# Hybrid decoder trunk on one core: gate groups and branch projections token by channel, both layers written out, the merge transposed onto its old layout

## The chip, the cores and the metric

The kernel runs on one core of a Trainium2 chip. The metric is device time in microseconds (us) of one execution, the median of several runs. The engines are named as in the profile: PE (TensorE; PEld is its weight load), DVE (VectorE), ACT (ScalarE), POOL (GpSimd), SP (SyncE, which here issues nearly all DMAs).

## What is computed

256 tokens of width 1024 go through two layers and a last RMSNorm. Cut to what matters here:

```
for l in range(2):
    h = rms_norm(x, norm_mix_g[l])
    proj = h @ w_in[l]                      # 1024 x 7492: u, va, q, k, v, index, cb, cc, cx, six gate groups of 512
    ya = gmlp_spatial(u, va, ws, bs)        # 512 wide
    yb = dsa_attention(q, k, v, ...)        # top 64 keys of each query, 4 heads
    yc = cb * conv3(cc * cx)                # 512 wide
    g  = sigmoid(gates)                     # 3 x 1024
    merged = g[0] * (ya @ w_proj_a) + g[1] * (yb @ w_proj_b) + g[2] * (yc @ w_proj_c)
    x = x + merged @ w_out
    h = rms_norm(x, norm_ffn_g[l])
    x = x + hier_moe(h, ...)                # 32 experts, 1024 x 512 x 1024, two for each token
return rms_norm(x, norm_final_g)
```

All is float32. The products of the mixing part are made of three products of rounded parts (high times high, high times low, low times high).

## The kernel before

**One layer** has a mixing part, a router and an expert part, and each engine runs its own program for it, in a hardware loop over the layer (`Fori(0, DEPTH) as l`: L434 on SP, L562 on POOL, L582 on ACT, L797 on DVE, L1201 on PE). Since `l` is in a register, each wait on a semaphore counts up from a value that a register instruction works out.

**Weights.** `ring` has 12 slots of 1 MB. In mixing SP loads weights into seven of them (`MIX_RING`); a load waits until the product that read the slot seven loads before is done. ACT rounds each slot to its high part (`high`, L636, into four more slots), DVE subtracts that for the low part (`low`, L813). A high part waits until the product that read the one four before is done.

**Mixing on PE.** `group(g)` (L1247) makes one group of 512 columns of `w_in`, from two slots, over 8 chunks of the 1024 input channels. Groups go by turns to psA and psB. Two orientations are in use, told apart by `token_major` (L1248): the first five groups (index, q, k, v, va) hold a 128-token piece of `hT` in the array and stream 512 weight columns; u, cx, cc, cb and the six gate groups hold 128 weight columns and stream 256 tokens, so their result has channels on the partitions. In both a `product` (L1218) is three matmuls:

```
def product(o, xs, ws, weights_stationary, start, stop):
    for i, (a, b) in enumerate(TERMS):
        first, second = (ws[b], xs[a]) if weights_stationary else (xs[a], ws[b])
        ins = te.matmul(o, first, second, start=start and i == 0, stop=stop and i == len(TERMS) - 1)
    return ins
```

Between the groups stand the small products of attention and of the spatial gate. After the gate groups come six branch projections (`for k in range(N_PROJ)`, ya, yb, yc for the first 512 channels, then for the other 512), with the weights in the array and 256 tokens streamed. DVE multiplies each by its gate (L1013) and adds (L1016) into `merged`, 8 chunks of channels by 256 tokens. ACT rounds each half of it to `merged_high` (L645), DVE makes `merged_low` (L1002), and PE multiplies both with `w_out` (two parts of the sum times two halves of the columns), which DVE adds to `x` (L1031).

**Router and experts.** DVE works out the top groups and experts, PE makes ranks, and a table tells for each pair of experts which tokens it takes. An inner hardware loop (L1508 on PE, L1167 on DVE, L726 on ACT, L500 on SP) runs over the pairs of experts, 16 in each layer with these inputs. A pair reads 12 slots (12 MB): PE gathers tokens (L1427), multiplies with gate and up (L1439) and down (L1451), and scatters by a 0/1 matrix (L1465, L1466); DVE adds to `x` (L1117). SP loads the next pair's slot when PE has freed it (`pair_freed`), six stages of two slots to a pair.

**The end of a layer** on DVE: the last two additions to `x`, then the layer loop's register instruction and branch, then at the loop's head the sum of squares of the next layer's norm (L828).

Of the kernel before, what the change touches and what calls it, by code (L numbers as in the profile page):

```python
# [29 lines left out]
P = 128  # L30
# [20 lines left out]
def build_trunk(nc, x_in, positions, norm_mix_g, norm_ffn_g, norm_final_g, w_in, gmlp_ws, gmlp_b, conv_w,  # L51
                w_proj_a, w_proj_b, w_proj_c, w_out, router_group_w, router_group_b,
                router_expert_w, router_expert_b, expert_w_gate, expert_w_up, expert_w_down, out):
    _, S, D = x_in.shape
# [87 lines left out]
    with ExitStack() as ctx:  # L142
# [6 lines left out]
        def rounded(name):  # L149


            offset, shape = place[name]
            return nc.alloc_sbuf_tensor_at(name + "_parts", shape, F32R, offset=offset)
# [34 lines left out]
        k_tok = share1[:, 1024:2048].rearrange("p (t n) -> p t n", t=NT)  # L188
        merged = share1[:, :].rearrange("p (c s) -> p c s", c=KC)
        qT = xn[:, 0:1024].rearrange("p (h s) -> p h s", h=HEADS)  # L190
# [8 lines left out]
        hT_high = rounded("hT")  # L199
        merged_high, merged_low = hT_high, rounded("share1")[:, :].rearrange("p (c s) -> p c s", c=KC)  # L200
        xn_parts = rounded("xn")
# [6 lines left out]
        hid = share1[:, 1536:2048]  # L208
        gate_parts = rounded("gates")
        y_high, y_low = [gate_parts[:, i].rearrange("p m s -> p (m s)").rearrange("p (n w) -> p n w", n=2) for i in (0, 3)]  # L210
# [135 lines left out]
        branch_act = sem("branch_act")  # L346
        merged_act = sem("merged_act")
        act_out = sem("act_out")
        idxT_act = sem("idxT_act")
# [77 lines left out]
        def sync_program(sp):  # L427
# [5 lines left out]
            sp.dma_start(rows[DEPTH * KC:, :], conv_w.rearrange("l k (c p) -> (l k c) p", p=P)).then_inc(rows_landed, 16)  # L433
            with sp.Fori(0, DEPTH) as l:  # L434

# [98 lines left out]
        def pool_program(pool):  # L534
# [25 lines left out]
            for k in range(STAGES):  # L560
                gp.memset(credit[:, k:k + 1], 0.0).then_inc(pair_freed, 1)
            with pool.Fori(0, DEPTH) as l:  # L562

                pool.wait_ge(wsT_act, l + 1)
                alone(pool)
                gp.affine_select(out=wsT[:, :, :], in_=wsT[:, :, :], compare_op=ALU.is_ge, fill=0.0, base=0,
                                 pattern=[[0, HEADS], [1, P]], channel_multiplier=-1).then_inc(tri_done, 1)


        def scalar_program(act):  # L570
# [10 lines left out]

            with act.Fori(0, DEPTH) as l:  # L582
                act.wait_ge(pairs_known, l + 1)
# [59 lines left out]
                def merged_part(half):  # L643
                    act.wait_ge(merged_done, l * 2 + half + 1)
                    sc.activation(merged_high[:, 4 * half:4 * half + 4, :], merged[:, 4 * half:4 * half + 4, :],  # L645
                                  ACT.Copy).then_inc(merged_act, 1)

# [100 lines left out]
        def vector_program(dve):  # L748
# [47 lines left out]

            with dve.Fori(0, DEPTH) as l:  # L797
                linked = [0]
# [200 lines left out]
                def merged_part(half):  # L999
                    dve.wait_ge(merged_act, l * 2 + half + 1)  # L1000
                    part = slice(4 * half, 4 * half + 4)
                    v.tensor_tensor(merged_low[:, part, :], merged[:, part, :], merged_high[:, part, :],  # L1002
                                    ALU.subtract).then_inc(merged_low_dve, 1)
# [3 lines left out]
                for half in range(2):  # L1007
                    dst = merged[:, 4 * half:4 * half + 4, :].rearrange("p (b h) s -> p b (h s)", b=2)
                    t2 = tmp[:, :].rearrange("p (b n) -> p b n", b=2)
# [184 lines left out]
        def tensor_program(pe):  # L1194
# [5 lines left out]
            pe.wait_ge(setup_done, 1)  # L1200
            with pe.Fori(0, DEPTH) as l:  # L1201
                pe.wait_ge(pairs_known, l + 1)
# [43 lines left out]
                def group(g):  # L1246

                    token_major = g in (G_QI, G_Q, G_K, G_V, G_VA)  # L1248
                    n = N_IDX if g == G_QI else WB
# [116 lines left out]


                for k in range(N_PROJ):
                    n = N_IN + k
                    p = PAD + 2 * N_IN + k  # L1370
                    branch = k % 3
                    if k == 0:
                        pe.wait_ge(branch_low_dve, l * 3 + 3)
                    w = split(p)
                    free_result(n)
                    for m in range(4):
                        for c in range(4):
                            ins = product((psA, psB)[n % 2][:, m // 2, (m % 2) * S:(m % 2 + 1) * S],
                                          [part[:, c, :] for part in (branch_high[branch], branch_low[branch])],
                                          [wp[:, c, m * P:(m + 1) * P] for wp in w], True, c == 0, c == 3)  # L1380
                    ins.then_inc(mixed, 1)

                for part in range(2):
                    for half in range(2):
# [6 lines left out]
                        for t in range(NT):  # L1391
                            for c in range(4):
                                m = 4 * part + c
                                ins = product((psA, psB)[n % 2][:, t, :], [h[:, m, t * P:(t + 1) * P] for h in (merged_high, merged_low)],
                                              [wp[:, c, :] for wp in w], False, m == 0, m == KC - 1)
                        if part == 1:
                            ins.then_inc(mixed, 1)
# [158 lines left out]
```

## Time and profile before

| | us |
|---|---|
| median of 3 runs | 1511.23 (1511.0 to 1513.61) |
| the profiled execution, its device time | 1510.52 |
| its span, first to last instruction | 1508.4 |
| TensorE's mean granted clock in it | 0.981 |
| PE, DVE, ACT busy | 1428.3, 557.2, 423.8 |

The device time lies 2.1 us above the span of the same execution, and the median 0.7 us above that execution. In the chain of waits a row is: start in us, length in us, engine, what it writes and its line; "issue" is time in which the engine waited for nothing that the profile shows. In the timeline a row is: start, length, engine, line, operation, output, inputs, shapes, count, and in brackets idle time before it and who ended it.

### The profile page before, as it was taken

The page shows a single profiled execution, that of the slowest core. Times are in us where ns is not written, and L with a number is a line of the kernel's source. Part 1 is how long each engine was busy: PE and PEld are TensorE (multiplying, and loading weights), DVE is VectorE, ACT ScalarE, POOL GpSimd, SP SyncE. Part 2 cuts the span into 40 slices and gives each one's busy share as a digit, 9 for nine tenths or more (in the row PEclk, how much of TensorE's full clock was granted, in tenths as well). Part 3 has the DMA queues.
Part 4 walks back from the last instruction along what each step waited for, and adds up shares of the span by engine and source line. Part 5 has one row for each costly group of instructions (what it writes and reads, how often), then busy time and mean ns, then how long its engine had stood idle before and what let it go on. Part 6 is the DMA issues. An engine that isn't in the chain of part 4 may idle for free.

```text
span 1508.4 us, 22388 instructions
## 1 busy us (share of the span) xinstructions
PE 1428.3 (95%) x8295; PEld 902.0 (60%) x8296; DVE 557.2 (37%) x872; ACT 423.8 (28%) x531; POOL 7.4 (0%) x43
## 2 busy tenths in 40 slices
PE   6999999899999999999879999998999999999996
PEld 5899998544444444444368999985444444444443
DVE  6785355522212212221267754564222222221223
ACT  5544332312212212211254543332221221221121
POOL 1000000000000000000000000000000000000000
PEclk9999999899999999999989999998999999999999
DMA  7544354899999999999935344548999999999995
GB/s 268 186 157 168 129 207 168 326 420 422 421 423 421 421 423 421 421 422 422 403 122 177 135 154 159 203 162 359 419 422 422 422 422 422 421 422 422 421 422 219
DMA packets 100818, 489.31 MB, mean 324 GB/s; under 512 B 8686, under 2 KB 12054, under 8 KB 51608
## 3 DMA queue, kind: packets, MB, share of 16 engines
q1 hardware_dynamic: 99656, 488.20, 80.8%
q8 instruction: 36, 0.59, 0.2%
q10 hardware_dynamic: 1104, 0.34, 0.1%
q14 instruction: 22, 0.18, 0.0%
HBM read 487.46 MB, written 1.05 MB: 324 GB/s over the span
## 4 chain that ended last, share of the span: by engine, by line
PE 63%; DMA 25%; DVE 6%; issue 4%; ACT 1%; SPq 0%; DVEq 0%; POOL 0%; ACTq 0%; POOLq 0%
DMA ring<-in_expert_w_up_dram 25%; PE psB L1439 19%; PE psA L1218 14%; PE psB L1218 12%; PE psC L1451 8%; PE psA L1427 5%; PE psA L1465 1%; PE psA L1466 1%; DVE work L908 1%; DVE top L907 1%; DVE ring_parts L813 1%; PE psD L1493 1%; PE psC L1340 1%; PE psC L1408 0%; PE psC L1339 0%
## 5 line engine op out<-in xcount | busy, mean ns | idle before, releaser
L1439 PE MATMUL psB<-ring,share 128*64 128x512 f32 x2048 | 462.8, 597 | 18.4 <-DMA ring<-in_expert_w_up_dram 18.4
L1439 PEld LDWEIGHTS psB<-ring,share 128*64 128x64 f32 x2048 | 141.9, 137 | 291.6 <-issue 271.0
L1451 PE MATMUL psC<-ring,share 128*64 128x512 f32 x1024 | 226.8, 595 | 0.0
L813 DVE TENSOR_TENSOR ring_parts<-ring,ring_parts 128x2048 fp32r<-128x2048 f32 (+1 forms) x80 | 176.8, 2249 | 69.1 <-ACT ring_parts L636 68.1
L636 ACT ACTIVATE ring_parts<-ring 128x2048 fp32r<-128x2048 f32 (+1 forms) x80 | 146.9, 1878 | 63.3 <-PE psA L1218 40.1
L1451 PEld LDWEIGHTS psC<-ring,share 128*64 128x64 f32 x1024 | 70.7, 137 | 131.7 <-issue 127.9
L1427 PEld LDWEIGHTS psA<-gates,xn 128*128 128x128 f32 x1088 | 131.4, 198 | 27.7 <-issue 26.0
L1117 DVE TENSOR_TENSOR x<-x,psA 128x1024 f32<-128x1024 f32 x62 | 75.7, 1221 | 192.0 <-PE psA L1466 192.0
L1427 PE MATMUL psA<-gates,xn 128*128 128x128 f32 x1088 | 140.3, 284 | 1.6 <-DVE gates L1086 1.6
L1218 PE MATMUL psA<-ring_parts 128*128 128x256 f32 (+2 forms) x416 | 126.2, 303 | 0.0
L1131 DVE TENSOR_TENSOR gates_parts<-psC,gates_parts 128x512 fp32r<-128x512 f32 x64 | 41.2, 686 | 222.8 <-ACT gates_parts L737 222.8
L1218 PE MATMUL psA<-hT_parts,ring_parts 128*128 128x256 f32 x640 | 117.4, 286 | 5.3 <-DVE ring_parts L813 5.3
L1218 PE MATMUL psB<-hT_parts,ring_parts 128*128 128x256 f32 x640 | 120.5, 291 | 0.0
L1218 PE MATMUL psB<-ring_parts 128*128 128x256 f32 (+1 forms) x384 | 117.5, 306 | 0.0
L737 ACT ACTIVATE gates_parts<-psC 128x512 fp32r<-128x512 f32 x64 | 34.7, 595 | 262.9 <-PE psC L1451 262.9
L1218 PEld LDWEIGHTS psA<-hT_parts,ring_parts 128*128 128x128 f32 x640 | 100.8, 194 | 6.1 <-issue 6.1
L1218 PEld LDWEIGHTS psB<-hT_parts,ring_parts 128*128 128x128 f32 x640 | 103.4, 199 | 0.4 <-issue 0.4
L1127 DVE SCALAR_TENSOR_TENSOR share<-gates,psB 128x512 f32<-128x512 f32 x32 | 23.9, 747 | 198.0 <-PE psB L1439 197.6
L1110 DVE TENSOR_TENSOR share<-psA,g_ffn 128x512 f32<-128x512 f32 x68 | 47.0, 691 | 95.8 <-PE psA L1427 95.8
L1218 PEld LDWEIGHTS psA<-ring_parts 128*128 128x128 f32 x416 | 79.9, 192 | 2.5
L729 ACT ACTIVATE gates<-psD 64x1 f32<-64x1 f32 x64 | 10.6, 165 | 249.0 <-PE psD L1482 248.6
L1218 PEld LDWEIGHTS psB<-ring_parts 128*128 128x128 f32 x384 | 75.3, 196 | 2.5
(310 smaller groups left out, 1300.3 us busy)
## 6 DMA issues: line engine op xcount, KB each, us to landing
ring<-in_expert_w_gate_dram SPq DMA_DIRECT2D x128, 1024.0 KB, 20.3
ring<-in_expert_w_up_dram SPq DMA_DIRECT2D x128, 1024.0 KB, 21.4
ring<-in_expert_w_down_dram SPq DMA_DIRECT2D x128, 1024.0 KB, 20.0
ring<-in_w_in_dram SPq DMA_DIRECT2D x56, 1024.0 KB, 7.0
ring<-in_w_out_dram SPq DMA_DIRECT2D x8, 1024.0 KB, 5.6
ring<-in_w_proj_a_dram SPq DMA_DIRECT2D x4, 1024.0 KB, 6.6
ring<-in_w_proj_b_dram SPq DMA_DIRECT2D x4, 1024.0 KB, 6.1
ring<-in_w_proj_c_dram SPq DMA_DIRECT2D x4, 1024.0 KB, 6.2
```

The costliest lines, as they stand in the source:

```text
L636: sc.activation(high_and_low(p)[0], mix_slot(p), ACT.Copy).then_inc(high_act, 1)
L737: sc.activation(y_high[:, n, :], psC[:, n, :], ACT.Copy).then_inc(y_act, 1)
L813: v.tensor_tensor(low_part, mix_slot(p), high_part, ALU.subtract).then_inc(low_dve, 1)
L907: link(v.max(top8[:, :], left[:, 0:nk]), True)
L1110: v.tensor_tensor(xT[:, 4 * b:4 * b + 4, :], psA[:, b, :].rearrange("p (c n) -> p c n", c=4), g_ffn[:, 4 * b:4 * b + 4].unsqueeze(2).to_br ...
L1117: v.tensor_tensor(x[:, t, :].rearrange("p (b n) -> p b n", b=2), x[:, t, :].rearrange("p (b n) -> p b n", b=2), (psB if last and t else ps ...
L1127: v.scalar_tensor_tensor(hid, silu, slot_w, psB[:, 1, :], ALU.mult, ALU.mult).then_inc(hid_done, 1)
L1131: v.tensor_tensor(y_low[:, n, :], psC[:, n, :], y_high[:, n, :], ALU.subtract).then_inc(y_dve, 1)
L1218: ins = te.matmul(o, first, second, start=start and i == 0, stop=stop and i == len(TERMS) - 1)
L1427: ins = te.matmul(psA[:, b, (c % 4) * P:(c % 4 + 1) * P], xn[:, o:o + P], sel[:, t].rearrange("p j n -> p (j n)"), start=t == 0, stop=t == ...
L1439: ins = te.matmul(psB[j * BLK:(j + 1) * BLK, o, :], xT[:, 4 * half + c, j * BLK:(j + 1) * BLK], w[:, c, :], start=half == 0 and c == 0, st ...
L1451: ins = te.matmul(psC[j * BLK:(j + 1) * BLK, n, :], hidT[:, 2 * k + c, j * BLK:(j + 1) * BLK], w[:, c, n * 512:(n + 1) * 512], start=k == ...
```

## The change

The gate groups are made token by channel like the first five groups (a 128-token piece in the array, 512 weight columns streamed), and so are the six branch projections. `merged` then has tokens on its partitions. Since the products with `w_out` need channels there, PE transposes each half of `merged` with the identity matrix into psC and psD, eight transposes of 128x128 to a half: the first half behind the fourth projection, the second behind the first quarter of the `w_out` product. ACT and DVE take `merged_high` and `merged_low` from psC and psD, where they took them from `merged` in SBUF, and `merged_low` moves from the place of `merged` to that of two gates that are used up. On every engine the hardware loop over the layer is a loop of the program's text, so that both layers are written out and `l` is a constant; the loops over the pairs stay.

```
-            with sp.Fori(0, DEPTH) as l:
+            for l in range(DEPTH):
...
-            with pool.Fori(0, DEPTH) as l:
+            for l in range(DEPTH):
...
-            with act.Fori(0, DEPTH) as l:
+            for l in range(DEPTH):
...
                 def merged_part(half):
-                    act.wait_ge(merged_done, l * 2 + half + 1)
-                    sc.activation(merged_high[:, 4 * half:4 * half + 4, :], merged[:, 4 * half:4 * half + 4, :],
-                                  ACT.Copy).then_inc(merged_act, 1)
+                    act.wait_ge(merged_ps, l * 2 + half + 1)
+                    sc.activation(merged_high[:, 4 * half:4 * half + 4, :].rearrange("p (b c) s -> p b (c s)", b=2),
+                                  (psC, psD)[half][:, :, :], ACT.Copy).then_inc(merged_act, 1)
...
-            with dve.Fori(0, DEPTH) as l:
+            for l in range(DEPTH):
...
                 def merged_part(half):
                     dve.wait_ge(merged_act, l * 2 + half + 1)
-                    part = slice(4 * half, 4 * half + 4)
-                    v.tensor_tensor(merged_low[:, part, :], merged[:, part, :], merged_high[:, part, :],
+                    v.tensor_tensor(merged_low[half].rearrange("p (b c) s -> p b (c s)", b=2), (psC, psD)[half][:, :, :],
+                                    merged_high[:, 4 * half:4 * half + 4, :].rearrange("p (b c) s -> p b (c s)", b=2),
                                     ALU.subtract).then_inc(merged_low_dve, 1)
...
-                    dst = merged[:, 4 * half:4 * half + 4, :].rearrange("p (b h) s -> p b (h s)", b=2)
+                    dst = merged[:, :, 512 * half:512 * half + 512]
...
-            with pe.Fori(0, DEPTH) as l:
+            for l in range(DEPTH):
...
-                    token_major = g in (G_QI, G_Q, G_K, G_V, G_VA)
+                    token_major = g in (G_QI, G_Q, G_K, G_V, G_VA) or g >= G_GATE0
...
+                def merged_transposes(half):
+
+                    pe.wait_ge(merged_done, l * 2 + half + 1)
+                    for c in range(4):
+                        for t in range(NT):
+                            o = (c % 2) * S + t * P
+                            ins = te.transpose((psC, psD)[half][:, c // 2, o:o + P],
+                                               merged[:, t, (4 * half + c) * P:(4 * half + c + 1) * P], ident[:, :])
+                    ins.then_inc(merged_ps, 1)
+
                 for k in range(N_PROJ):
...
-                    for m in range(4):
+                    for t in range(NT):
                         for c in range(4):
-                            ins = product((psA, psB)[n % 2][:, m // 2, (m % 2) * S:(m % 2 + 1) * S],
-                                          [part[:, c, :] for part in (branch_high[branch], branch_low[branch])],
-                                          [wp[:, c, m * P:(m + 1) * P] for wp in w], True, c == 0, c == 3)
+                            ins = product((psA, psB)[n % 2][:, t, :],
+                                          [part[:, c, t * P:(t + 1) * P] for part in (branch_high[branch], branch_low[branch])],
+                                          [wp[:, c, :] for wp in w], False, c == 0, c == 3)
                     ins.then_inc(mixed, 1)
+                    if k == 3:
+                        merged_transposes(0)
...
-                                ins = product((psA, psB)[n % 2][:, t, :], [h[:, m, t * P:(t + 1) * P] for h in (merged_high, merged_low)],
+                                o = slice(t * P, (t + 1) * P)
+                                ins = product((psA, psB)[n % 2][:, t, :], [merged_high[:, m, o], merged_low[part][:, c, o]],
                                               [wp[:, c, :] for wp in w], False, m == 0, m == KC - 1)
+                        if part == 0 and half == 0:
+                            merged_transposes(1)
```

How the instructions stand, at two places. First PE at the end of the fourth branch projection (the first of the second half of the channels; `ring_parts` are the rounded weights, `xn_parts` and `uT_parts` the parts of ya, `share` is `merged`). Before, its last matmuls and the first of the fifth projection:

```order
L1218 MATMUL psA<-uT_parts,ring_parts 128x256
L1218 MATMUL psA<-xn_parts,ring_parts 128x256 x2
L1218 MATMUL psA<-uT_parts,ring_parts 128x256
L1208 REGISTER_ALU
L1228 REGISTER_ALU
L1218 MATMUL psB<-ybT,ring_parts 128x256 x2
```

and of the change:

```order
L1219 MATMUL psA<-ring_parts,uT_parts 128x512
L1219 MATMUL psA<-ring_parts,xn_parts 128x512 x2
L1219 MATMUL psA<-ring_parts,uT_parts 128x512
L1375 MATMUL psC<-ident,share 128x128 x8
L1219 MATMUL psB<-ring_parts,ybT 128x512 x2
L1219 MATMUL psB<-ring_parts,xn_parts 128x512
```

The matmuls are 512 wide and half as many, and the eight transposes stand between the two projections; the register instructions ahead of the waits are gone.

Second DVE from the last row of its pair loop to the norm that follows. Before (L797 is the layer loop's branch, and what follows it in the text is the norm after the last layer; the next layer's is at the loop's head):

```order
L1167 COMPARE_AND_BRANCH
L1117 TENSOR_TENSOR x<-x,psA 128x1024
L1117 TENSOR_TENSOR x<-x,psB 128x1024
L1173 ISA
L797 REGISTER_ALU
L797 COMPARE_AND_BRANCH
L1184 ISA xn,ss<-x 128x1024
```

and of the change, behind the first layer:

```order
L1168 COMPARE_AND_BRANCH
L1118 TENSOR_TENSOR x<-x,psA 128x1024
L1118 TENSOR_TENSOR x<-x,psB 128x1024
L1174 ISA
L829 ISA xn,ss<-x 128x1024
L829 ISA ss 128x1
L787 TENSOR_SCALAR var<-ss 128x2
```

The second layer's norm now stands directly behind the first layer's last addition, with no branch between them.

## Rows read from the trace of the kernel before

**Rows 1.** The page: span, and the chain that ended last by engine.

```profile
span 1508.4 us, 22388 instructions
...
PE 63%; DMA 25%; DVE 6%; issue 4%; ACT 1%; SPq 0%; DVEq 0%; POOL 0%; ACTq 0%; POOLq 0%
```

**Rows 2.** Chain of waits in the expert parts: start us, us, what.

```profile
349.26 7.02 PE psB L1439 x32
...
377.37 7.02 PE psB L1439 x32
...
1304.52 25.40 DMA ring<-in_expert_w_up_dram
...
1334.37 25.41 DMA ring<-in_expert_w_up_dram
```

**Rows 3.** Busy time of 284 to 288 us; columns PE, PEld, DVE, ACT, POOL, PEclk, DMA share, GB/s.

```profile
284.00:288.00 4.00, 4.00 (x21) 1.46 (x21) 0.69 (x1) 0.00 (x0) 0.00 (x0) 1.00 0.02 6
```

**Rows 4.** Timeline of SP's DMA issues: the second pair's first load.

```profile
288.36 1.03 SPq L445 DMA_DIRECT2D ring<-in_expert_w_gate_dram  x2
```

**Rows 5.** Chain of waits in the first mixing part: group q, two gate groups, a projection, a w_out quarter.

```profile
25.59 10.89 PE psB L1218 x48
...
159.89 13.59 PE psB L1218 x96
...
185.00 11.52 PE psB L1218 x96
...
219.45 5.65 PE psB L1218 x48
...
247.50 5.44 PE psA L1218 x24
```

**Rows 6.** Timeline of PE: group cx starts after idle time.

```profile
90.08 0.50 PE L1218 MATMUL psA<-hT_parts,ring_parts 128*128 128x256 f32 x2 [2.63 <-DVE ring_parts L813]
```

**Rows 7.** Timeline of ACT and DVE during the fourth gate group: high and low parts of two slots.

```profile
175.38 3.71 ACT L636 ACTIVATE ring_parts<-ring 128x2048 fp32r<-128x2048 f32 x2
...
177.32 4.50 DVE L813 TENSOR_TENSOR ring_parts<-ring,ring_parts 128x2048 fp32r<-128x2048 f32 x2 [0.58 <-ACT ring_parts L636]
```

**Rows 8.** Timeline of PE: eight transposes of q and the next group.

```profile
60.49 1.03 PE L1292 MATMUL psD<-ident,share 128*128 128x128 f32 x8
61.28 0.71 PE L1218 MATMUL psA<-ring_parts,hT_parts 128*128 128x512 f32 x2
```

**Rows 9.** Timeline of ACT and DVE at the merge: merged_high, last addition of the second half, merged_low.

```profile
229.02 1.06 ACT L645 ACTIVATE hT_parts<-share 128x1024 fp32r<-128x1024 f32 x1 [7.61 <-DVE share L1016]
...
243.33 1.23 DVE L1016 TENSOR_TENSOR share<-share,tmp 128x1024 f32<-128x1024 f32 x1
...
249.09 1.22 DVE L1002 TENSOR_TENSOR share_parts<-share,hT_parts 128x1024 fp32r<-128x1024 f32 x1
```

**Rows 10.** Chain of waits from the first layer into the second, on DVE.

```profile
750.48 1.23 DVE x L1117
...
751.89 5.59 issue
...
757.61 0.13 DVE xn L828
```

**Rows 11.** Chain of waits from the second layer into the last norm, on DVE.

```profile
1498.58 1.22 DVE x L1117
...
1500.04 0.11 DVE xn L1184
```

**Rows 12.** Timeline of ACT from the first layer into the second.

```profile
746.43 1.28 ACT L580 ACT_TABLE_LOAD   x1 [0.17 <-issue]
```

**Rows 13.** Chain of waits between two linked DVE instructions of the top-k scores.

```profile
57.20 0.03 issue
```

**Rows 14.** Busy time around the transposes of q and behind the spatial gate; columns as in rows 3.

```profile
60.00:64.00 4.00, 4.00 (x23) 3.38 (x22) 2.83 (x13) 3.31 (x3) 0.00 (x0) 1.00 0.50 135
160.00:164.00 4.00, 4.00 (x19) 4.00 (x20) 3.98 (x3) 0.00 (x0) 0.00 (x0) 0.50 0.02 4
```

More of the change, by code:

```diff
@@ L188, in build_trunk @@
         k_tok = share1[:, 1024:2048].rearrange("p (t n) -> p t n", t=NT)
-        merged = share1[:, :].rearrange("p (c s) -> p c s", c=KC)
+        merged = share1[:, :].rearrange("p (t n) -> p t n", t=NT)
         qT = xn[:, 0:1024].rearrange("p (h s) -> p h s", h=HEADS)
@@ L199, in build_trunk @@
         hT_high = rounded("hT")
-        merged_high, merged_low = hT_high, rounded("share1")[:, :].rearrange("p (c s) -> p c s", c=KC)
+        gate_parts = rounded("gates")
+        merged_high, merged_low = hT_high, (gate_parts[:, 0], gate_parts[:, 2])
         xn_parts = rounded("xn")
@@ L208, in build_trunk @@
         hid = share1[:, 1536:2048]
-        gate_parts = rounded("gates")
         y_high, y_low = [gate_parts[:, i].rearrange("p m s -> p (m s)").rearrange("p (n w) -> p n w", n=2) for i in (0, 3)]
@@ L347, in build_trunk @@
         merged_act = sem("merged_act")
+        merged_ps = sem("merged_ps")
         act_out = sem("act_out")
```

## The prediction

> **What bounds the kernel now.** I read the span and the chain by engine first [rows 1]: 1508.4 us, of which 63% is PE, 25% DMA, 6% DVE. The device time of this execution is 1510.52 us, the median 1511.23; all sums below are differences, so they apply to either.
>
> In the expert parts two paces show [rows 2]. While the ring still holds a reserve, a pair takes 377.37 - 349.26 = 28.11 us, set by PE. Later it takes 1334.37 - 1304.52 = 29.85 us, and the chain lies in the DMA of the twelve slots. The slower of the two, the DMA, decides the end. When does that stream start? The ring is full before the experts begin: from 284 to 288 us the DMAs move 6 GB/s [rows 3], and the next load is issued only at 288.36 us, when PE has freed the first stage of the first pair [rows 4]. So the end of a layer is PE's first expert product plus about 15 x 29.85 us and a tail. Whatever is gained before the experts moves the end by the same amount, and nothing that this change does inside the pair loops matters unless a pair grows past 29.85 us.
>
> In the mixing parts the chain runs on PE from group to group [rows 5]. A group of 48 matmuls, 512 wide, takes 10.89 us (0.227 us each); a gate group of 96, 256 wide, takes 11.52 us (0.120 us each). The columns are the same 24,576, so the difference of 0.63 us is what each matmul costs beside its columns. The one place where PE waits for another engine among the groups is before group cx, 2.63 us for DVE's low part, behind the top-k work [rows 6]; the change does not touch this chain of work.
>
> **The change, part by part.**
>
> *Gate groups.* Six in each layer go from 11.52 to 10.89 us [rows 5]: 12 x 0.63 = 7.6 us gained. ACT and DVE must keep up. The tightest place is the fourth gate group: the low parts for the fifth are ready at 177.32 + 4.50 = 181.8 us [rows 7], and the fifth starts at 185.00 [rows 5], 3.2 us later; with shorter groups 2.6 us are left. Sigmoid, gates and multiplications keep their sizes.
>
> *Branch projections.* 48 matmuls in 5.65 us become 24 as wide as those of a `w_out` quarter, 5.44 us [rows 5]: 12 x 0.21 = 2.5 us gained.
>
> *Transposes.* Eight between two groups cost 61.28 - 60.49 = 0.79 us from start to start [rows 8]. Four times eight are added, all on PE's path: 3.2 us lost. They bring two handovers. Take T as the end of the fourth projection. Before, the first half of `merged` is complete at 228.99 us (rounding starts at 229.02 [rows 9]), 1.7 us before the fourth projection ends (219.45 + 2 x 5.65 = 230.75, the second having ended at 219.45 [rows 5]); with projections 0.2 us shorter it stays 1.3 us early, so PE does not wait at T. Transposes end at T + 0.8, ACT's rounding (1.06) at T + 1.9, DVE's low part (1.22) at T + 3.1 [rows 9]. Queued behind them: ACT's high parts of two `w_out` slots (1.85 each [rows 7]) end at T + 5.6, DVE's low parts (2.25 each [rows 7]) at T + 8.3, then the products of the fifth projection, which has been ready since T + 6.2. Its multiplication and addition (1.23 each [rows 9]) end at T + 10.7, those of the sixth (ready at T + 11.7) at T + 14.2. PE reaches the second transposes after two projections and a quarter of `w_out`, at T + 0.8 + 3 x 5.44 = T + 17.1: 2.9 us of room. It needs the second low part at T + 23.4; DVE has two low parts of weights until T + 18.7, ACT's rounding ends at T + 19.0, the low part at T + 20.2: 3.2 us of room. If the cover were gone, a handover would cost 0.8 + 1.06 + 1.22 = 3.1 us each. I take 0.
>
> *The layer loop.* Once in the run, DVE goes back to the loop's head. Its last addition ends at 751.71 us; then come 5.59 us in which it waits for nothing, and the norm starts at 757.61 [rows 10]: 5.90 us. At the end of the second layer the same kind of norm stands straight behind the addition and starts at 1500.04, 0.24 us after 1499.80 [rows 11]. The difference, 5.7 us, is on the path, since everything of the second layer hangs on this norm. ACT goes round the same loop and loses 0.17 us [rows 12], so the loss depends on how much program an engine must go back over. In the change there is no way back: I take the 5.7 us as gained whole. The ends are 0 (the code of the second layer must be fetched anyway and might be late) and 5.7.
>
> *Register instructions.* On DVE 200 of them stand in the old text and 14 in the new. Between two linked instructions of the top-k work 0.03 us pass, with a register instruction between them [rows 13]; they run while the engine works. I take 0; the gain is at most the 0.03, times some 70 links on the path, 2 us.
>
> Sum: -7.6 - 2.5 + 3.2 - 5.7 = -12.6 us. The profiled execution would take 1497.9, the median 1498.6 us.
>
> **What the Trainium skill says, beside the rows.** The rows show 0.120 and 0.227 us from matmul to matmul [rows 5]. The Trainium skill, page "TensorE: Matmul & The Clock Gate", section "Back-to-back issue gap", gives columns over 2.4 GHz plus 2.5 ns, so about 0.109 and 0.216 us. By that a gate group would gain only 0.1 us; it is the third rival. The trace does not agree with it in size, and the trace has both forms in this very code, so I go by the trace.
>
> **The rivals.**
>
> 1. *The stall on DVE stays in another place.* The second layer's code is new text, and its first instructions might arrive late behind the pair loop. For it: nothing but the stall's own size. Against it: the last norm, also behind a pair loop, came in 0.24 us [rows 11]. Then -6.9 us: 1504.3 us.
>
> 2. *The transposes cost PE its clock.* Behind the spatial gate, with its many small matmuls, the granted clock is 0.50 (1.2 GHz) at 160 to 164 us [rows 14], and the gate group there takes 13.59 instead of 11.52 us [rows 5], 2.1 us. If each of the four transpose places did this, 8.3 us would be lost: 1506.9 us. Against it: around the eight transposes of q the clock stays 1.00 at 60 to 64 us [rows 14]. The Trainium skill, same page, section "PE-mode transpose", says that transposes do not count as busy time for the clock; by that each added place is a danger, and the trace shows that one place of 0.79 us among long groups was harmless.
>
> 3. *The gain of wide matmuls is not there.* The 0.120 us would have to belong to something else than the width. With gains of 0.1 us for each gate group and 0.05 for each projection, 1.8 us in all, the sum is -1.8 + 3.2 - 5.7 = -4.3: 1506.9 us. Against it: 5.65 and 5.44 us stand within 30 us of each other with the same engines around them.
>
> 4. *Slower: a pair loop now loses what the layer loop lost.* The written-out text places each pair loop elsewhere. If DVE's way back in it cost 5.59 us [rows 10] as the layer loop's did, behind the last low part of a pair, a pair would take up to 28.11 + 5.59 = 33.7 us, over the 29.85 of the DMA by 3.85 us; 30 periods give +115.5, with the rest of the sum -12.6: 1614 us. It decides from 29.85 - 28.11 = 1.74 us of exposed loss a pair on, and from 2.2 us on it makes the kernel slower than before. Against it: neither of the two shows such a loss in the old program's pairs [rows 2], the loop is some 20 instructions long, and its text is unchanged. The Trainium skill, page "Runtime: NRT & Kernel Launch", section "Instruction fetch mechanics", says that only a jump out of a window of two blocks has to fetch; a short loop would lose only if it lay across such a window.
>
> **How the numbers follow.** The forecast has 0.70, with its own range of 1495.5 to 1501.5 us (0 to 3 us of room eaten up at a handover or by the clock's changes, and up to 3 us gained from shorter register work and a better lie of the clock at the start of the second layer). Rival 1 has 0.11, rival 2 0.07, rival 3 0.03, rival 4 0.04, and 0.05 is for a gain beyond the forecast's range, down to 1493.5 (all register work gone and the wait before cx shorter). The range from 1493.5 to 1505.0 holds the forecast, rival 1 and the greater gain. A measurement of this kernel can tell about 0.2%, 3.0 us, from no change. The forecast and rivals 1 to 3 all lie more than 3.0 us below 1511.2, though rivals 2 and 3 only just: faster 0.94, within 0.2% 0.02, slower 0.04.
>
> **What would show it.** In the changed kernel the gate groups should take 10.9 us in the chain, the projections 5.44, each group of eight transposes under 0.9 with no idle time of PE ahead of them, and DVE's norm of the second layer should start within 0.3 us of the last addition. The first expert product should come some 3.4 us earlier in the first layer and 12.6 us earlier in the second, the pairs keeping 28.1 and 29.85 us. The prediction is wrong if the wait before the second norm is still above 2 us, if the granted clock drops behind the transposes, if PE waits for `merged_done`, or if the period of a pair exceeds 29.85 us.

## The result, and the profile after

| | before | after |
|---|---|---|
| median, us (runs, on the same chip) | 1512.12 (4) | 1497.30 (4: 1495.47, 1495.62, 1498.98, 1499.93) |
| ratio, 95% interval | | 0.9900 (0.9881 to 0.9920) |
| profiled execution, device time, us | 1510.52 | 1495.47 |
| its span, us; granted TensorE clock | 1508.4; 0.981 | 1493.7; 0.983 |

The kernel is 1.0% faster: 15.1 us by the ratio, with 12.1 to 18.0 us as its interval. The forecast was 12.6 us. The four runs fall into two pairs 4 us apart, the faster two with a mean granted clock of 0.983, the slower two with 0.981, and the profiled one is the fastest of them. Which places can differ by so much is told below; the slower pair has no trace.

The page of the changed kernel, where [rows 1] stood:

```profile
span 1493.7 us, 19746 instructions
...
PE 65%; DMA 24%; DVE 8%; issue 2%; ACT 1%; SPq 0%; POOL 0%; DVEq 0%; ACTq 0%; POOLq 0%
```

The share of "issue" (time in which an engine waits for nothing that the profile shows) has fallen from 4% to 2%. The instructions are fewer by 2,642: half the matmuls of the gate groups and projections with their weight loads, and the register work.

The chain of waits of the changed kernel, first layer (start us, us, what), where [rows 5] stood; below it the two expert paces of [rows 2], and the first expert product of each layer:

```profile
25.35 10.92 PE psB L1219 x48
...
159.65 13.11 PE psB L1219 x48
...
183.64 10.88 PE psB L1219 x48
...
205.40 5.59 PE psB L1219 x24
...
216.56 5.56 PE psB L1219 x24
222.12 5.61 PE psA L1219 x24
227.73 0.87 PE psC L1375 x8
228.60 5.58 PE psB L1219 x24
...
251.58 5.44 PE psB L1219 x24
257.02 5.45 PE psA L1219 x24
...
281.72 7.02 PE psB L1455 x32
...
346.70 7.02 PE psB L1455 x32
...
374.81 7.02 PE psB L1455 x32
...
1019.43 7.02 PE psB L1455 x32
...
1319.90 25.36 DMA ring<-in_expert_w_up_dram
...
1349.72 25.38 DMA ring<-in_expert_w_up_dram
```

A gate group takes 10.88 us, where it took 11.52. A projection takes 5.56 to 5.61, where it took 5.65: less of a gain than the 5.44 forecast, which the quarter of `w_out` at 251.58 does reach. The eight transposes are in the chain with 0.87 us. The pairs keep 374.81 - 346.70 = 28.11 us and 1349.72 - 1319.90 = 29.82 us. The first expert product stands at 281.72 us in the first layer (before 284.30) and at 1019.43 in the second (before 1032.97), 2.6 and 13.5 us earlier, where 3.4 and 12.6 had been expected.

The layer boundary in the same chain, where [rows 10] stood:

```profile
745.10 0.23 PE psA L1482
...
746.97 1.22 DVE x L1118
748.20 0.02 issue
748.22 1.23 DVE xn L829
```

The 5.59 us of "issue" have become 0.02. The row at 745.10 is a matmul of the scatter at full clock; it comes up again below.

The handover at the merge, on the timelines of PE, then of ACT and DVE (start us, us, engine, line, operation, idle time before and what ended it), where [rows 9] stood:

```profile
227.57 1.03 PE L1375 MATMUL psC<-ident,share 128*128 128x128 f32 x8
228.36 0.71 PE L1219 MATMUL psB<-ring_parts,ybT 128*128 128x512 f32 x2
...
245.05 1.04 PE L1375 MATMUL psD<-ident,share 128*128 128x128 f32 x8
```

```profile
224.85 1.23 DVE L1017 TENSOR_TENSOR share<-share,tmp 128x1024 f32<-128x1024 f32 x1
...
228.64 1.03 ACT L646 ACTIVATE hT_parts<-psC 128x1024 fp32r<-128x1024 f32 x1 [10.06 <-PE psC L1375]
...
229.77 1.23 DVE L1002 TENSOR_TENSOR gates_parts<-psC,hT_parts 128x1024 fp32r<-128x1024 f32 x1 [0.71 <-ACT hT_parts L646]
...
241.11 1.23 DVE L1017 TENSOR_TENSOR share<-share,tmp 128x1024 f32<-128x1024 f32 x1
...
247.19 1.22 DVE L1002 TENSOR_TENSOR gates_parts<-psD,hT_parts 128x1024 fp32r<-128x1024 f32 x1 [0.33 <-ACT hT_parts L646]
```

No PE row here has a bracket, so PE waited neither for `merged` nor for its transposed parts. The first half of `merged` is complete at 224.85 + 1.23 = 226.08 us, 1.5 us before PE comes to it (1.3 had been worked out); the second at 242.34, 2.7 us before 245.05 (2.9). The second low part ends at 248.41, and the third quarter of `w_out`, which reads it, begins only at 251.58: 3.2 us of room, as worked out.

The clock around the added transposes, and behind the spatial gate, where [rows 14] stood (us, PE, PEld, DVE, ACT, POOL, PEclk, DMA share, GB/s):

```profile
152.00:156.00 4.00, 4.00 (x17) 2.71 (x15) 0.00 (x0) 3.32 (x2) 0.00 (x0) 0.70 0.96 349
156.00:160.00 4.00, 4.00 (x12) 2.88 (x12) 0.31 (x1) 0.00 (x0) 0.00 (x0) 0.50 0.46 169
...
226.00:230.00 4.00, 4.00 (x23) 3.37 (x22) 1.53 (x3) 1.36 (x2) 0.00 (x0) 1.00 1.09 384
230.00:234.00 4.00, 4.00 (x19) 3.22 (x18) 3.50 (x3) 3.27 (x2) 0.00 (x0) 1.00 0.54 205
```

The transposes do not lower the clock. It does fall, to 0.50 (1.2 GHz), in the spatial gate, where it fell before the change too.

### The profile page after: what moved, and what is told of

It is laid out like the page before. It is cut to its first block, busy times and chain, and to the rows that moved or that the text cites. A ratio compares the mean times of both kernels' runs of the same rounds, so it can differ in the third digit from the quotient of the medians.

```text
span 1493.7 us, 19746 instructions
## 1 busy us (share of the span) xinstructions
PE 1421.6 (95%) x7463; PEld 859.2 (58%) x7463; DVE 557.0 (37%) x871; ACT 423.5 (28%) x530; POOL 7.5 (0%) x43
## 4 chain that ended last, share of the span: by engine, by line
PE 65%; DMA 24%; DVE 8%; issue 2%; ACT 1%; SPq 0%; POOL 0%; DVEq 0%; ACTq 0%; POOLq 0%
DMA ring<-in_expert_w_up_dram 24%; PE psB L1455 19%; PE psA L1219 14%; PE psB L1219 11%; PE psC L1467 8%; PE psA L1443 5%; DVE ring_parts L814 2%; PE psA L1481 2%; PE psA L1482 1%; DVE work L909 1%; DVE top L908 1%; PE psD L1509 1%; PE psC L1341 1%; PE psC L1340 1%; PE psC L1424 1%
## 5 line engine op out<-in xcount | busy, mean ns | idle before, releaser
L1455 PE MATMUL psB<-ring,share 128*64 128x512 f32 x2048 | 462.5, 596 | 17.9 <-DMA ring<-in_expert_w_up_dram 17.9
L1219 PE MATMUL psA<-ring_parts,hT_parts 128*128 128x512 f32 (+1 forms) x448 | 134.8, 383 | 2.0 <-DVE ring_parts L847 2.0
L1219 PE MATMUL psB<-ring_parts,hT_parts 128*128 128x512 f32 x384 | 121.6, 398 | 0.0
L1219 PE MATMUL psA<-ring_parts 128*128 128x512 f32 (+2 forms) x320 | 109.2, 341 | 0.0
L1219 PE MATMUL psB<-ring_parts 128*128 128x512 f32 (+1 forms) x288 | 99.7, 346 | 0.0
L1219 PEld LDWEIGHTS psA<-ring_parts,hT_parts 128*128 128x128 f32 x448 | 83.7, 191 | 17.3 <-issue 2.7
L1219 PEld LDWEIGHTS psB<-ring_parts,hT_parts 128*128 128x128 f32 x384 | 73.4, 193 | 16.2 <-issue 1.1
L735 ACT ACTIVATE share<-psD 128x512 f32<-128x512 f32 x32 | 19.1, 597 | 189.8 <-PE psD L1509 189.8
L1219 PEld LDWEIGHTS psA<-ring_parts 128*128 128x128 f32 x320 | 61.3, 192 | 6.2
```

The costliest lines, as they stand in the source:

```text
L1455: ins = te.matmul(psB[j * BLK:(j + 1) * BLK, o, :], xT[:, 4 * half + c, j * BLK:(j + 1) * BLK], w[:, c, :], start=half == 0 and c == 0, st ...
```

## What had to be told apart

The theory: the gain is the sum of independent terms on one path, namely the way back of DVE's layer loop, the number of matmuls in the gate groups and projections, and the transposes as a cost. The rivals: the new orientation, not the number of matmuls, makes the groups shorter; the loop's gain needs all engines, or hides a wait of PE for new code; the transposes cost more through the clock or their handovers than by their own length. Two things were open besides: why a projection stopped at 5.57 us, and where the 2 to 3 us beyond the sum come from. Times below are ratios to the kernel before, run on the same chip, times 1512 us.

## The experiments

**The layer loop alone, on all engines.** The kernel before, with this edit at the loops of SP, POOL, ACT, DVE and PE:

```
-            with dve.Fori(0, DEPTH) as l:
+            for l in range(DEPTH):
```

> The kernel before with the layer loop written out on all five engines, and nothing else changed. My theory: DVE's way back to the loop's head is all that this removes, so the norm of the second layer starts within 0.3 us of the last addition instead of 5.9 us, and the whole is 5.7 us shorter than before, give or take the 2 us that the clock's lie moves. Rival (the wait moves elsewhere): below 2 us. Second rival (the register instructions also cost): 8 us or more, and then the links of the top-k work pass in less than 0.03 us.

Ratio 0.9954 (0.9939 to 0.9969): 7.0 us less. The norm starts 0.03 us behind the addition, in the chain:

```profile
749.17 1.23 DVE x L1117
...
750.43 1.22 DVE xn L828
```

The wait before group cx also shrank, from 2.63 us [rows 6] to 2.42. That wait stands behind the linked top-k instructions on DVE, where the written-out text has no register instructions.

**The orientation alone.** The changed kernel with the five hardware loops put back.

> The changed kernel with the layer loop put back as a hardware loop on all engines: gates, projections and transposes alone. My theory, from the groups read in the changed trace: 12 x 0.63 + 12 x 0.08 - 4 x 0.87 = 5.0 us shorter than before, with 5.6 us of wait back at DVE's loop edge. Rival (the two parts of the change need each other): 9 us or more shorter, since the changed profile was 14.7 us below the old one and the loop is worth 5.7.

Ratio 0.9957 (0.9940 to 0.9974): 6.5 us less. The stall is back in the chain, and PE again waits 2.63 us before cx:

```profile
749.15 1.23 DVE x L1118
...
750.55 5.25 issue
...
755.94 0.13 DVE xn L829
```

The two halves of the change add up to 7.0 + 6.5 = 13.5 us, within the interval of the whole.

**DVE's loop alone.** The kernel before, with the edit above on DVE only.

> The kernel before with the layer loop written out on DVE alone; PE, ACT, SP and POOL keep their hardware loops. My theory: all of the loop's gain is DVE's, 5.7 us. Rival: PE, whose loop is the longest, has a wait of the same size hidden under DVE's, so that the gain is smaller than with all five loops written out; PE's transposes would then start later than 0.1 us behind ACT's scaled x.

Ratio 0.9957 (0.9944 to 0.9971): 6.5 us less, so DVE alone brings nearly all of it. In the chain (the first row is the last matmul of the scatter):

```profile
752.10 0.44 PE psB L1466
...
752.56 1.23 DVE x L1117
...
753.82 1.22 DVE xn L828
```

PE, still in its hardware loop, got no later: its work behind this norm starts 4.22 us after the norm, against 4.14 us where its loop is written out too. No wait of PE reaches the path. PE is idle there for 5.5 us in either case, though, so a wait of its own of up to that length could lie hidden in it, and this run can't rule it out. The scatter's matmul takes 0.44 us here, at a granted clock of 0.50 from 750 to 752 us, and 0.23 in the changed kernel's profile at 1.00.

**The gate groups alone, 512 wide.** The kernel before, with the condition below; the projections and `merged` stay as they were.

```
-                    token_major = g in (G_QI, G_Q, G_K, G_V, G_VA)
+                    token_major = g in (G_QI, G_Q, G_K, G_V, G_VA) or g >= G_GATE0
```

> The kernel before with only the six gate groups made token by channel, 512 wide; the projections stay channel by token, so gates and projections no longer fit each other in the multiplication (that part of the computation is changed). My theory: each of the 12 gate groups takes 10.89 us instead of 11.52, 7.6 us in all. Rival (the width is not what costs): no change. The clock behind the spatial gate may fall earlier or later, by 1 to 2 us in either layer, which the granted clock shows.

Ratio 0.9934 (0.9916 to 0.9953): 10.0 us less, 7.1 to 12.7 by the interval, which the 7.6 just lies in. The groups in the chain are the measure, and they take what the changed kernel's take:

```profile
184.71 10.88 PE psB L1218 x48
...
217.88 5.65 PE psB L1218 x48
```

**The same orientation, 256 wide.** The gate groups token by channel, each row of 512 cut in two:

```
+                    if g >= G_GATE0:
+                        for m in range(NT):
+                            for q in range(2):
+                                cut = slice(256 * q, 256 * q + 256)
+                                for c in range(KC):
+                                    ins = product(ps[:, m, cut], [h[:, c, m * P:(m + 1) * P] for h in (hT_high, hT_low)],
+                                                  [wp[:, c % 4, cut] for wp in w[c // 4]], False, c == 0, c == KC - 1)
```

> As e4 (gate groups token by channel, projections not, so that gates and projections don't fit each other in the multiplication, which changes that part), but each gate product is issued in two halves of 256 columns: 96 matmuls of 256 with the orientation of the 48 of 512. My theory, that each matmul costs some 13 ns beside its columns: the groups take 11.52 us again, as in the kernel before, and the gain of e4 (0.63 us a group) is gone. Rival (the orientation gains, the tokens in the array instead of the weights): the groups keep 10.89 us.

Ratio 1.0003 (0.9993 to 1.0014): no gain at all. The groups are back at their old length:

```profile
186.53 11.52 PE psB L1218 x96
```

In these groups the orientation is worth nothing, and the number of matmuls accounts for the whole gain. 48 matmuls fewer for the same 24,576 columns save 0.64 us, 13 ns each. The Trainium skill, page "TensorE: Matmul & The Clock Gate", section "Back-to-back issue gap", has 2.5 ns beside the columns, for a matmul by itself. For a stream of weight loads and matmuls the same section gives about 131 ns for 512 columns. By the 2.5 ns the twelve groups would save an estimated 1.4 us; the runs do not agree, nor does the trace with the 131 ns: it has 227.

**No transposes.** The changed kernel without them; ACT and DVE read `merged` in SBUF.

```
-                    if k == 3:
-                        merged_transposes(0)
...
-                        if part == 0 and half == 0:
-                            merged_transposes(1)
```

> The changed kernel without the transposes of the merge: merged_high and merged_low are taken from the merged sums in SBUF as they lie, tokens on the partitions, so the product with w_out is made of the wrong operand (that part of the computation is left out). My theory: 4 x 0.87 = 3.5 us shorter than the changed kernel, all on PE, and no other group changes; against the kernel before some 16 to 18 us. Rival (the handovers cost as well): more than 4.5 us shorter.

Ratio 0.9881 (0.9860 to 0.9903), 0.0019 under the changed kernel's: 2.9 us. The two intervals overlap (0.9881 to 0.9920 is the changed kernel's), so the chain has to give the price. Here are the first projection and the last quarter of `w_out` in it:

```profile
204.50 5.59 PE psB L1219 x24
...
254.30 5.45 PE psA L1219 x24
```

From the start of the one to the end of the other PE needs 259.75 - 204.50 = 55.25 us. In the changed kernel it needs 262.47 - 205.40 = 57.07. The difference is 1.82 us for two places, and it is the same in the second layer: 3.6 us in all, of which 3.5 are the transposes' rows of 0.87 and the rest is 0.04 us at each place in the groups around them. Nothing is left for the handovers.

**The transposes three times.**

```
-                    for c in range(4):
+                    for c in [0, 1, 2, 3] * 3:
```

> The changed kernel with each of the 32 transposes of the merge issued three times into the same place: 16 more at each of the four places. My theory: 0.1 us a transpose, so each place takes 2.4 us instead of 0.79, 6.4 us in all over the changed kernel, and the granted clock stays at 2.4 GHz. Rival (transposes cost PE its clock): the clock falls to 1.2 GHz behind at least one of the places, and the groups behind it take over 1 us longer.

Ratio 0.9944 (0.9925 to 0.9963), 0.0044 over the changed kernel's: 6.7 us. The timeline of PE gives 228.72 - 226.18 = 2.54 us for 24 transposes, 1.75 more than the 0.79 for eight, and four times 1.75 is 7.0 us. The windows show the clock at 1.00 behind them:

```profile
226.18 2.78 PE L1375 MATMUL psC<-ident,share 128*128 128x128 f32 x24
228.72 0.48 PE L1219 MATMUL psB<-ring_parts,ybT 128*128 128x512 f32 x1
```

```profile
226.00:230.00 4.00, 4.00 (x32) 3.69 (x31) 1.22 (x1) 1.00 (x2) 0.00 (x0) 1.00 0.94 338
230.00:234.00 4.00, 4.00 (x19) 3.25 (x18) 3.36 (x2) 3.63 (x3) 0.00 (x0) 1.00 0.21 88
```

So a transpose here costs little more than its own length, 0.11 us, and even 24 in a row among long groups leave the clock alone. The Trainium skill, same page, section "PE-mode transpose", says that a transpose does not count as busy for the clock gate. Should that hold, these places were still too short to matter; no run here separates the two.

**A projection that reads other parts.** The changed kernel, with `hT_high` in place of both parts of the branch:

```
-                                          [part[:, c, t * P:(t + 1) * P] for part in (branch_high[branch], branch_low[branch])],
+                                          [hT_high[:, 4 + c, t * P:(t + 1) * P] for _ in range(2)],
```

> The changed kernel with the branch projections reading four chunks of hT in place of the high and low parts of the branches (the branch results then do not reach the output, that part of the computation is left out). In the changed kernel a projection takes 5.57 us, 0.232 us a matmul, where the gate groups and the w_out quarters take 0.227. Theory: it is the place or the kind of the operand in the array that costs 0.13 us a projection, and from hT, as the gate groups use it, a projection takes 5.44 us. Rival: it is the stage (the weights' four chunks, the work beside it), and 5.57 us stay. Either way the whole changes by 1.6 us at most, which one round does not tell; the groups in the trace decide.

```profile
209.43 5.44 PE psA L1219 x24
```

Now the projections reach 5.44 us (ratio 0.9894, 0.9866 to 0.9923, which can't tell so little from the changed kernel). The missing 0.13 us belongs to the branch parts as operands in the array: where they lie, or that high and low part are two tiles, since here both were one. Which of these it is stays open. The gate groups and the quarters of `w_out` also read high and low parts from two tiles, and they have no such loss. The loss is alike for all three branches, 5.56 to 5.61 us.

**An earlier low part on DVE.** The remaining wait of PE among the groups is the one before cx, [rows 6] before. In the changed kernel DVE's low part for slot unit 6 was put ahead of the statistics of v, which wait for ACT:

```
+                low(*unit_slots(6))
                 dve.wait_ge(act_out, l * len(on_act) + 1 + on_act.index(G_VA))
...
                 variance(mv[:, :, 1], 1.0, link)
-                low(*unit_slots(6))
```

> The changed kernel with DVE's low parts for group cx taken ahead of the statistics of v instead of behind them. PE's only wait among the groups is there, 2.4 us in each layer. My theory: the wait shrinks by the statistics' 2.0 us, 4.0 us in all, and nothing behind becomes late. Rival: the masks and the low parts for the next group, now later on DVE, make PE wait at group cc instead, and less than 1 us is gained.

Ratio 0.9873 (0.9856 to 0.9891), 0.0027 or 4.1 us below the changed kernel's. The first row is the changed kernel, the second this one:

```profile
89.65 0.48 PE L1219 MATMUL psA<-hT_parts,ring_parts 128*128 128x256 f32 x2 [2.39 <-DVE ring_parts L814]
```

```profile
87.70 0.48 PE L1219 MATMUL psA<-hT_parts,ring_parts 128*128 128x256 f32 x2 [0.40 <-DVE ring_parts L814]
```

Twice 1.99 us is 4.0, as measured, and no wait came up behind it. The intervals of the two ratios touch (0.9881 to 0.9891), so the rows carry this finding and the times agree with it.

**Matmuls to hold the clock, before the ranks.** 18 idle matmuls ahead of the wait for `members`, in the changed kernel:

```
+                def keep_busy(n):
+                    for _ in range(n):
+                        te.matmul(psD[:, 1, :], ones_r[:, :], ybT[:, 0:2, :].rearrange("p h s -> p (h s)"), start=True, stop=True)
...
+                keep_busy(18)
                 pe.wait_ge(members, l + 1)
```

> The changed kernel with 18 idle-time matmuls of 512 columns (4.1 us) on PE ahead of its wait for the experts' member table, where PE is idle 4.6 us, written to an unused half of psD. Theory: the granted clock falls in that idle time and the gather (32 matmuls) takes 5.2 to 5.6 us in the changed kernel; kept busy, PE keeps 2.4 GHz and the gather takes 3.6 us, so each layer is some 1.5 to 2 us shorter, 3 to 4 us in all. Rival: the clock falls anyway, or the added matmuls outlast the wait and make the ranks late; then no gain.

Ratio 0.9876 (0.9853 to 0.9899). In the first layer the clock fell all the same, only later, inside the gather:

```profile
272.00:276.00 4.00, 2.54 (x13) 1.76 (x11) 3.39 (x23) 1.33 (x2) 0.00 (x0) 1.00 1.01 426
276.00:280.00 4.00, 3.94 (x23) 3.94 (x24) 2.07 (x10) 1.28 (x1) 0.00 (x0) 0.66 1.02 424
```

In the second layer the clock fell while the idle matmuls themselves ran (0.61 from 1008 to 1012 us) and was back at 1.00 for the gather, which took 3.8 us instead of 5.2. From the router's transposes to the first expert product this made 16.5 us instead of 17.7 in the second layer, and 17.6 instead of 17.9 in the first. That is one execution, and the interval overlaps the changed kernel's; a gain isn't shown.

**Matmuls to hold the clock, between the layers.** 20 of them ahead of the second layer's norm transposes (`if l > 0: keep_busy(20)`).

> The changed kernel with 20 idle-time matmuls of 512 columns (4.5 us) on PE between the last scatter of the first layer and the second layer's norm transposes, where PE is idle 5.7 us. Theory: the index group of the second layer took 9.1 us instead of 7.2 because the granted clock was still 1.2 GHz; kept busy, PE makes it in 7.2 us and the transposes before it faster, 2 to 3 us in all. In runs in which the clock happened to return early there is less to gain. Rival: no effect, or under 1 us.

Ratio 0.9905 (0.9885 to 0.9926): no gain. The eight-transpose groups took about 1.0 us each instead of 1.9, but PE then stood before the next thing that was late:

```profile
748.04 5.12 PE L1233 MATMUL psD<-ybT,ones_r 128*128 128x512 f32 x20
...
758.33 0.54 PE L1219 MATMUL psA<-ring_parts,hT_parts 128*128 128x324 f32 x2 [2.68 <-DVE ring_parts L847]
```

DVE sets that start: it makes the low parts of the index group's weights first and those of `hT` behind them, so that the index group starts 8.79 us behind the start of the norm here and in the changed kernel alike, whatever the transposes take. The index group itself still took 8.7 us.

**All three.** The earlier low part and both sets of idle matmuls.

> The changed kernel with the earlier low parts of e8 and the idle-time matmuls of e9 and e10 together. If the three gains are independent, they add up: 4 + 3 to 4 + 2 to 3, so 9 to 11 us below the changed kernel, about 1486 to 1488 us. Rival: the clock's places are shared, and only e8's 4 us remain.

Median 1491.81 us, ratio 0.9848 (0.9828 to 0.9867): clearly below the changed kernel's (0.9881 to 0.9920), by 7.9 us, where 9 to 11 had been expected. Its interval overlaps that of the earlier low part alone, which is 3.8 us above it. The gather takes 5.47 us in both layers, where it took 5.65 and 5.26 in the changed kernel, and the spans of the two profiled executions are alike (1490.9 and 1490.4 us). So it stays open whether the idle matmuls bring anything. The version to keep is the changed kernel with the low part moved: one line, 1492.97 us, and a gain that the rows explain.

## Why the prediction was right, point by point

The sum of the forecast against the profiles before and after:

| term | forecast, us | measured, us | from |
|---|---|---|---|
| gate groups | -7.6 | -7.7 | 12 x (11.52 - 10.88) |
| projections | -2.5 | -1.0 | 12 x (5.65 - 5.57) |
| transposes | +3.2 | +3.5 | 4 x 0.87; 3.6 against the run without them |
| handovers | 0 | 0 | no wait of PE |
| DVE's layer loop | -5.7 | -5.9 | 5.90 - 0.02 |
| register instructions | 0 | -0.7 | 2 x (2.63 - 2.39), first group 18.21 to 18.02 |
| sum | -12.6 | -11.8 | span: -14.7 |

- *Gate groups*: right in size, and the reason given (what each matmul costs beside its columns) was tested against its rival by the 256-wide groups. Rival 3, that the gain of wide matmuls is not there, fell. The prediction sized it by the 2.5 ns; the section gives this figure for a matmul by itself, and these groups are streams.
- *Projections*: the mis-sized term. The step took a projection as equal to a quarter of `w_out` because both have 24 matmuls of that width; a projection's operands in the array cost it another 0.13 us. The change gains 0.08 us a projection, not 0.21, so 1.0 us instead of 2.5.
- *Transposes*: 0.87 us each place against 0.79. From start to start the transposes take 0.79 us in the changed kernel too; the group behind them is then 0.08 us longer, and the sum left that out. Rival 2, the clock, fell by the windows and by the tripled transposes.
- *Layer loop*: right. Writing out DVE's loop alone removed the loss of 5.9 us, and it did not come back in another place (rival 1: the norm starts 0.02 us after the addition). The 0.24 us in front of the last norm [rows 11], which the sum had kept, went too: in the changed kernel, and with DVE's loop written out alone, it starts 0.02 us behind the last addition. The way back cost 5.25 to 5.59 us on DVE and 0.17 on ACT [rows 12]; no run tests what makes the difference, and so the prediction's reason, how much program an engine goes back over, stays argued. The Trainium skill, page "Runtime: NRT & Kernel Launch", section "Instruction fetch mechanics", says that a jump out of the fetched window has to wait for the program, and gives no price. The trace agrees as far as it goes: it shows the loss and where it lies, not the fetch.
- *Register instructions*: "they run while the engine works" was not quite so. The wait before cx is shorter by 0.24 us where DVE's loop is written out, and 2.63 us again where it isn't.
- *Pair loops*: rival 4 fell; the paces are 28.11 and 29.82 us. And what was gained before the experts did arrive at the end: the first expert product of the second layer is 13.5 us earlier, and the end 14.7.

The remaining 14.7 - 11.8 = 2.9 us is in none of these terms. Some 1.8 of it can be put down to TensorE's clock: gathers -1.0 and -0.3, scatter of the first layer -1.0, cx of the second layer -1.5, groups behind the two spatial gates +0.2 and -1.3 beside their gain, against the spatial gate of the first layer +1.4 and the index group of the second +1.9, with the second spatial gate at -0.2. Another 0.2 is DVE's way out of the layer loop in front of the last norm. The last 0.9 us arises behind the first expert product of the second layer, where the DMAs come to set the pace (1453.74 - 1032.97 us before, 1439.27 - 1019.43 after, to the last load in the chain), and no run shows why.

Another execution lays the clock's places differently, and so the median (1497.3) lies 1.8 us above the profiled run's time. A forecast by the terms of the table gives 1511.2 - 11.8 = 1499.4 us, 2.1 us above the measured median, which is about what one of the clock's places varies by. So the mechanism was right, but that the forecast of 1498.6 came within 1.3 us of the measured median is partly luck: the projections gained 1.5 us less than forecast, the register instructions 0.7 us more, and the clock and the expert part gave some 2.7 us in the profiled execution that no term had.

## What to carry to other kernels

Count matmuls, not only columns: for the same columns, each matmul saved was worth 13 ns in these float32 groups, whichever operand is in the array. 32 transposes at 0.11 us each were then a fair price, 3.6 us against the 8.7 us gained in twelve gate groups and twelve projections. A hardware loop that is gone round once may stand on the critical path with the way back of one engine, here DVE's; read the gap before the first instruction of the second turn, and write out that loop. Before taking a group's length from another group of the same shape, look whether it reads the same tiles.

## What the runs showed of the hardware

- The granted clock can fall to 1.2 GHz while PE is busy all the time: in the spatial gate (4.00 us busy of 4.00, clock 0.70, then 0.50), with few and small matmuls in the window (x17, x12). In the traces of all kernels here that stage took 6.6 to 9.1 us, and the group behind it 1.5 to 3 us more than its length at full clock. Where PE had been idle before, group cx took 11.6 or 13.1 us and the index group 7.2 or about 9.
- These places are likely what makes one kernel's runs differ by 3 to 5 us. That is not shown, since only one execution of each kernel has a trace; in the first layer's expert part the two traces, before and after, agree within 0.1 us from the first expert product to the scatter (462.85 and 462.88 us).
- Idle matmuls ahead of such a place did not reliably hold the clock: in three of four gathers it fell behind them, inside the gather, and in the fourth while they ran.
- 24 matmuls with the same shapes took 5.44 or 5.57 us, 0.227 or 0.232 each, depending on the tiles in the array. Why is open.
